# Query projections of the second head pair, issued before the branch ahead of them is closed

## The reference

```python
o_m = dense_latent_attention(q_m, k_m, v_m, kc_m, vc_m, MLA_SCALE)            # "mla", 8 heads
o_s = window_latent_attention(q_s, k_s, v_s, kc_s, vc_s, sink, SWA_SCALE)     # "swa", 8 heads, window 128
o_a = dense_latent_attention(q_a, k_a, v_a, kc_a, vc_a, AX_SCALE)             # "ax", 8 heads
x = x + gate * merge_branches(o_m, o_s, o_a, z_m, z_s, z_a, g, lw)

# merge_branches
y_m = (o_m.reshape(B, T, MLA_WIDTH) * jax.nn.silu(z_m)) @ lw['w_o_mla']       # the same for swa and ax
y = sigmoid(g_m) * y_m + sigmoid(g_s) * y_s + sigmoid(g_a) * y_a
return y @ lw['w_out']
```

## Time and profile before

| what | value |
|---|---|
| median of three runs | 1842.52 us |
| the profiled execution's own time | 1838.8 us |
| its span, first to last instruction | 1836.7 us |
| TensorE busy | 1722.7 us, 94% |
| VectorE busy | 1093.4 us, 60% |
| ScalarE busy | 1050.6 us, 57% |
| GpSimd busy | 527.3 us, 29% |
| mean granted TensorE clock | 0.975 of full speed |

### The profile page before, as it was taken

The page is one execution under the profiler, slowest core; times in us unless marked ns, Lnnn a source line. Parts: engine busy times, 40 slices in busy tenths (PEclk is TensorE's granted clock), DMA queues, the critical chain, the costliest instruction groups (busy, mean ns, idle before and its releaser), DMA issues.

```text
span 1836.7 us, 27005 instructions
## 1 busy us (share of the span) xinstructions
PE 1722.7 (94%) x10554; PEld 1502.7 (82%) x10554; DVE 1093.4 (60%) x2185; ACT 1050.6 (57%) x1921; POOL 527.3 (29%) x300
## 2 busy tenths in 40 slices
PE   7999999899999999999999999989898989999897
PEld 2777888789898889888789977878787867888787
DVE  5534777765555565555866652677665455656544
ACT  3435777766665776765221533767766666776332
POOL 1523222122222222222322442332143222322342
PEclk9999999999999999999999998999999998999999
DMA  8111012111211111113545321112113121212542
GB/s 317 38 36 28 24 33 58 35 41 35 56 44 47 41 41 41 36 46 121 183 128 164 102 67 36 31 33 59 35 47 81 52 64 41 58 48 57 184 143 92
DMA packets 178526, 129.51 MB, mean 71 GB/s; under 512 B 21661, under 2 KB 167647, under 8 KB 178400
## 3 DMA queue, kind: packets, MB, share of 16 engines
q1 hardware_dynamic: 174242, 115.37, 22.1%
q10 hardware_dynamic: 2878, 8.24, 1.2%
q0 software_dynamic: 1280, 4.20, 0.7%
HBM read 123.58 MB, written 4.19 MB: 70 GB/s over the span
## 4 chain that ended last, share of the span: by engine, by line
PE 73%; DVE 11%; ACT 8%; POOL 3%; issue 3%; DMA 1%; SPq 0%; DVEq 0%; ACTq 0%; POOLq 0%
PE acc L1327 54%; PE wide L1383 6%; PE ptp L1403 6%; PE pv L1416 4%; PE pv L1417 3%; DVE nmax L1956 2%; DVE pt L1981 2%; ACT e L1647 2%; POOL w_lo L1771 1%; DMA w_raw<-in_ada_w 1%; POOL h_lo L1809 1%; ACT w_hi L1565 1%; DVE k_s L1519 1%; DVE k_m L1519 1%; ACT pt L1662 1%
## 5 line engine op out<-in xcount | busy, mean ns | idle before, releaser
L1771 POOL TENSOR_TENSOR w_lo<-w_raw,w_hi 128x1024 fp32r<-128x1024 f32 (+2 forms) x192 | 391.7, 2044 | 1142.3 <-ACT w_hi L1565 1142.1
L1327 PE MATMUL acc<-h_hi,w_hi 128*128 128x512 f32 (+2 forms) x1320 | 467.2, 355 | 20.4 <-POOL w_lo L1771 6.4
L1327 PE MATMUL acc<-h_hi,w_lo 128*128 128x512 f32 (+2 forms) x1320 | 463.4, 352 | 0.0
L1327 PE MATMUL acc<-h_lo,w_hi 128*128 128x512 f32 (+2 forms) x1320 | 459.7, 352 | 0.3 <-POOL h_lo L1809 0.3
L1662 ACT ACTIVATE pt<-ptp 128x512 fp32r<-128x512 f32 (+3 forms) x312 | 165.9, 563 | 244.4 <-PE ptp L1403 243.6
L1956 DVE TENSOR_REDUCE nmax<-wide 128x1 f32<-128x768 f32 (+3 forms) x240 | 189.8, 791 | 190.7 <-PE wide L1383 189.1
L1327 PEld LDWEIGHTS acc<-h_hi,w_hi 128*128 128x128 f32 (+1 forms) x1320 | 249.9, 189 | 62.2 <-issue 13.1
L1327 PEld LDWEIGHTS acc<-h_hi,w_lo 128*128 128x128 f32 (+1 forms) x1320 | 249.8, 189 | 33.9
L1327 PEld LDWEIGHTS acc<-h_lo,w_hi 128*128 128x128 f32 (+1 forms) x1320 | 247.4, 189 | 35.1 <-POOL h_lo L1809 0.5
L1654 ACT ACTIVATE e<-e,einv 128x768 f32<-128x768 f32 (+3 forms) x240 | 193.4, 806 | 54.0 <-DVE einv L1973 53.6
L1981 DVE TENSOR_TENSOR pt<-ptp,pt 128x512 fp32r<-128x512 f32 (+3 forms) x312 | 191.8, 640 | 48.3 <-ACT pt L1662 48.2
(11 more groups left out here) (212 smaller groups left out, 3120.6 us busy)
## 6 DMA issues: line engine op xcount, KB each, us to landing
w_raw<-in_w_in SPq DMA_DIRECT2D x102, 512.0 KB, 3.9
w_raw<-in_ada_w SPq DMA_DIRECT2D x48, 512.0 KB, 5.4
w_raw<-in_w_out SPq DMA_DIRECT2D x16, 512.0 KB, 3.8
w_raw<-in_w_in SPq DMA_DIRECT2D x16, 256.0 KB, 3.3
w_raw<-in_w_o_mla SPq DMA_DIRECT2D x16, 256.0 KB, 2.8
w_raw<-in_w_o_swa SPq DMA_DIRECT2D x16, 256.0 KB, 2.8
w_raw<-in_w_o_ax SPq DMA_DIRECT2D x16, 256.0 KB, 2.8
w_raw<-in_mla_w_uq SPq DMA_DIRECT2D x16, 144.0 KB, 2.3
```

What stands on the lines that cost most here:

```text
L1327: ins = nc.tensor.matmul(dst, lhs, rhs, start=first, stop=last)
L1771: nc.gpsimd.tensor_tensor(w_lo[s][:, 0:k], w_raw[s][:, 0:k], f(w_hi[s][:, 0:k]), ALU.subtract).then_inc(w_lo_ready, 1)
```

## The change

Two entries of the queue get other conditions. The second query pair of swa no longer waits for the z tile that needs the closed mla branch; it may run when the scores of the last mla head are issued and the first swa pair is done. The second query pair of ax no longer waits for the z tile that needs the closed swa branch, but for the last y tile of mla, which stands ahead of it in the queue.

```diff
@@ -783,8 +783,8 @@
             y_item(0, 2 * t)
             if t + 1 < KO:
                 z_item(1, t + 1)
-                item((SWA, t + 1), SWA, tile_cost, lambda s, t=t: t == 0 or (SWA, 2 * t - 1) in s, q_pair(SWA, t + 1),
-                     urgent=True, after=[("z", 1, 0), (SWA, t)])
+                item((SWA, t + 1), SWA, tile_cost, lambda s, t=t: (("mla", HEADS - 1) if t == 0 else (SWA, 2 * t - 1)) in s, q_pair(SWA, t + 1),
+                     urgent=True, after=[(SWA, t)])
                 y_item(0, 2 * t + 1)
@@ -798,7 +798,7 @@
             if t + 1 < KO:
                 z_item(2, t + 1)
                 item((AX, t + 1), AX, tile_cost, lambda s, t=t: t == 0 or (AX, 2 * t - 1) in s, q_pair(AX, t + 1),
-                     urgent=True, after=[("z", 2, 0), (AX, t)])
+                     urgent=True, after=[("y", 0, 2 * KO - 1) if t == 0 else ("z", 2, 0), (AX, t)])
             y_item(1, 2 * t + 1)
```

## The result

| | median of the runs | ratio to before, 95% interval | profiled execution: its span, mean clock |
|---|---|---|---|
| before | 1842.34 us (6 runs) | 1 | 1836.7 us, 0.975 |
| changed | 1853.53 us (6 runs) | 1.0055 [1.0033, 1.0077] | 1846.1 us, 0.968 |

The change makes the kernel 0.55% slower, 10 us, where 12 us less were forecast. The time lies above the range, which ended at 1843 us.

The account below looks back on a forecast made before the run. TensorE, busy 94%, was taken as the bound, with winnable waits on VectorE where branches end. Terms 2.0 + 0.4 + 6.7 + 4.6 - 2.2 + 2.6 - 2 = 12.1 us took 1842.5 to 1830.4 us; range 1819 to 1843 us.

Parts of the forecast that it names:

- First place: Layer 0, mla to swa: steps fill waits of 2.90 us, 0.9 us comes back; +2.0 us.
- VectorE +2.2 us of halves against -2.2 us of stall: Layer 0, mla to swa: new query halves add 2.2 us on VectorE, the `esink` stall of 2.2 us goes.
- lower bound of -0.2 us: Layer 0, mla to swa: the worth if the `esink` stall only moves.
- Second place: Layer 0, swa to ax: 3.15 us of waits filled, a wait of 2.7 us takes their place; +0.4 us.
- The clock behind both: Layer 0, swa to ax: if the clock falls behind the new wait, another 1.7 us are lost.
- new spells of lower clock: Whole kernel: a sign that the prediction is wrong, if they appear; no size given.
- Third place: Layer 1, mla to swa: waits of 1.11, 2.39, 1.02 and 2.14 us go; +6.7 us.
- longest wait: Layer 1, swa: the 5.32 us wait shrinks by 3.3 us, clock gives 1.3 us; +4.6 us.
- Fourth place: Layer 1, swa to ax: `statq` waits 1.71 us, splits add 0.5, -2.2 us; forced steps and clock spell behind go, +2.6 us.
- Elsewhere: All swa units get a little less filler: one more wait of about 1.1 us in each layer; -2 us.
- The rival "slower": All four places: rotation and halves lengthen the closing's chain, clock falls behind; 9.3 us slower, 1851.8 us; chance 8%.
- The rival "waits only exchanged": All ends: VectorE has the new pair's work, waits are only exchanged; 3.2 us gain, 1839.3 us; chance 25%.

Follow-up runs that it names:

- swa0: Kernel before with the new condition for swa in layer 0 only (first place); ratio to before 1.0020.
- keep_busy: Changed kernel with unused matmuls filling TensorE's waits ahead of the first swa and first ax product in layer 0; ratio to before 1.0013.
- swa1: Kernel before with the new condition for swa in layer 1 only (third place); ratio to before 0.9970.
- ax1: Kernel before with the new condition for ax in layer 1 only (fourth place); ratio to before 0.9994.
- layer1: Kernel before with both new conditions in layer 1 alone, layer 0 in the order of before; ratio to before 0.9979.
- og_twice: Kernel before, its order kept, with the low half of the closed branch's output made twice at layer 0's three closings; ratio to before 1.0121.

## Why the prediction was wrong, step by step

- **First place, +2.0 us: failed; measured about -5 us** (353 to 562 us, the changed kernel and swa0). The 2.90 us filled and the 0.9 us less work are right. The step "VectorE +2.2 us of halves against -2.2 us of stall" gave a wait of 2.4 us; it was 5.35 us. The exchange itself held (+0.21 us). What I had not counted is 1.42 us ahead of the sum (rotation and a new stall) and 1.20 us by which `og_lo` grew beside GpSimd's rotation. My lower bound of -0.2 us took the stall as moved, and no more.
- **Second place, +0.4 us: failed; measured about -8 us** (562 to 832 us). The wait came out at 4.51, not 2.7 us. The halves and the missing work were counted nearly right; what was missing is the 1.49 us by which the rotation and the slower sum put off `og_lo`. `og_lo` itself did not grow here.
- **The clock behind both** was a bound at the second place, 1.7 us, and missing at the first. It is the failed step with the largest price: 2.8 and 5.6 us by the work done at half clock (estimate); keep_busy got back 2.4 and 3.4 us. The prediction named new spells of lower clock as a sign of being wrong, and they came.
- **Third place and longest wait, +6.7 and +4.6 us: right in direction, too large.** All four waits of the earlier trace rows went. Against them stand 1.1 us (1.46 to 2.56), a new 0.89 us and a new 1.96 us, and the longest wait shrank by 1.3, not 3.3 us. Net 2.6 to 3.5 us of the 11.3 in three profiles; swa1 gave 0.30%, 5.5 us.
- **Fourth place, -2.2 and +2.6 us, net +0.4: the sign of the net is right, its parts are not.** The squares cost 0.69, not 1.71 us, and the 1.71 us and the spell behind it are gone; another spell, at 1532 to 1544 us, is longer. Net 1.6 to 3.2 us in three profiles, and nothing that ax1's 0.9994 can tell.
- **Elsewhere, -2 us: no such loss shows in layer 0 beyond the two places.** Behind them, from 386 to 562 us and from 634 to 832 us of before, the changed kernel gets back 2.6 and 4.9 us, since steps that ran early are missing there; the -5 and -8 us above include this.
- **The rival "slower"** (8%) had the mechanism: rotation and halves in the closing's chain, and the lower clock behind it. It put it at all four places; it holds for layer 0 alone. Its 1851.8 us is near the measured 1853.5 us by luck: it charges places of layer 1 that gained, and leaves the clock in layer 0 too small. I argued against it from the third place, where it does fail, and let that speak for the first two. The rival "waits only exchanged" has the sum of the waits nearly right (+4.2 us), not the clock.

## What to carry to other kernels

Where the clock is full behind a small wait, as at the first two places, filling it is worth its length at most; if the filler brings work to the engine that the next long wait ends on, add up that engine's chain from product to product, what it meets on GpSimd too, before counting a gain. The waits that grew to 5.35 and 4.51 us cost their length and then 2.8 and 5.6 us in clock; of the waits of 1 to 2 us here most cost only their length, but not all (behind the 1.71 us of the earlier trace rows the clock was at 0.72). Where such a wait can't be removed, useless matmuls in it kept the clock up.

## What the runs showed of the hardware

The lower clock lasted 6.8 us with the wait of 5.35 us and 13.7 us with that of 4.51 us, the part inside the wait counted, and cost more at the shorter one. Behind 1.42 and 0.66 us at 582 us it fell in some kernels (0.60 at 584 to 588 us in the changed one) and not in others with the same two rows (before, layer1, keep_busy), so single profiles carry a few us of chance. The Trainium skill, "TensorE: Matmul & The Clock Gate", section "Part 1: The HAM clock gate (the "warmup" mystery)", says that the clock follows how busy TensorE has been; keep_busy, whose filler computes nothing that is used, agrees. VectorE and GpSimd slowed each other both ways: `og_lo` 3.56 to 4.76 us, GpSimd's rotation 1.29 to 1.47 and 1.90 us, and in og_twice the splits 4.95 to 5.89 us.
